# First block's input projection of a fused two-block model: features as the outer loop in its first half

## The chip, the cores and the metric

One NeuronCore of a Trainium2 chip. The metric is the device time of one execution in microseconds. The whole program is one launch on one core; its inputs lie in HBM.

## The reference, cut to what matters

The program computes two "first blocks" (pooling and convolution mixers with adaptive modulation), then an FFN, a sparse attention mixer, two FFNs, a difference attention mixer and a last FFN, all for 256 tokens of width 1024. The change touches the first of the two first blocks (l = 0) alone:

```python
c_act = jax.nn.silu(c)                              # (1, 1024)
mod = c_act @ w_ada[l] + b_ada[l]                   # (1, 3072)
shift, scale, gate = jnp.split(mod, 3, axis=-1)
h = rms_norm(x, g_pre[l]) * (1.0 + scale[:, None, :]) + shift[:, None, :]
proj = h @ w_in[l]                                  # (1, 256, 3072)
u_a, b_a, c_a, gate_a, u_p, gate_p = jnp.split(proj, 6, axis=-1)
y_a = b_a * causal_depthwise_conv(c_a * u_a, w_conv[l]) * jax.nn.silu(gate_a)
y_p = causal_multiscale_pool(u_p, w_pool[l], pool_scale[l]) * jax.nn.silu(gate_p)
y = jnp.concatenate([y_a, y_p], axis=-1) @ w_out[l]
x = x + gate[:, None, :] * rms_norm(y, g_post[l])
```

## The kernel before, in words

**Precision.** Every large product is made of three passes in a fast f32 format: high part of the weight by high part of the activation, high by low, low by high. ScalarE makes the high part of a weight chunk (`split_hi`, L745: a copy into `whi`), VectorE the low part (`split_lo`, L1349: the difference into `wlo`). Small products (sums, transposes) are plain f32.

**The stream of weights.** `stream_items` (L90) writes out the order of all loads. Each item is 1 MiB and goes into one of three slots of `raw` (RAW = 3, L41). SyncE issues load r when `raw_done` has reached r - 2, which means that item r - 3 has been released (L433). Releases come from VectorE, in the order of the items: the low split of a weight chunk, or, for rows of `w_ada`, the multiplication by a scalar of `cact` and the addition to a row of sums in SBUF (`add_row`, L1355 and L1356; called from `accumulate_ada`). ScalarE needs for a high split that the chunk has landed and that TensorE is done with the chunk three before (`chunk_used`); TensorE needs the low split. VectorE, ScalarE and TensorE work their programs in order, so a release or a split that is ready still waits for what stands ahead of it in its engine's queue.

**Block 1 before.** The first 8 items are the rows of `w_ada[0]` for shift and scale (128 x 2048 each, rows of 8 KB). VectorE adds them up; TensorE sums the 128 partitions by 16 matmuls against ones (L2291), which gives all 16 columns of shift and scale; `modulation(0, 0)` (L1529 to L1531) makes shift and gain. Meanwhile x lands as the fourth transfer, ScalarE squares and scales it (L896, L901), GpSimd takes the power -0.5 (L516), TensorE transposes x (`turn`, L2087). ScalarE then applies gain and shift (`to_features`, L793), VectorE makes the high and low parts `hT_hi`, `hT_lo` (L1565, L1566). `keep_clock` (L2281) puts 3 and 2 matmuls of 512 f32 columns around the sums, whose result nobody reads.
The projection goes by 12 chunks of 256 columns of W_in, all 1024 features deep (rows of 1 KB), in the order of `IN1_ORDER`: 48 matmuls a chunk (`pooled_pair` for the first two, `cols_by_tokens` for the rest, L2122 to L2124), into rotating PSUM banks. After chunks there are hooks: windowed means of the pooling branch (L2314, L2315, they need `win_ready` from GpSimd), the mixing (L2321), the sums of the gate (L2273) and its spread over the partitions (L2330); on ScalarE the evictions, `gate` diagonal (L940) and taps; on VectorE `pooled_y` parts (L1583), the convolution (L1605) and the gating. From the third chunk on, the stream has after every chunk one item for later: 4 items of gate rows and 8 rows of `w_ada[1]`. The output product (`out_chunk` L2221 to L2223, `out_pair` L2239 to L2241) uses 4 chunks of W_out, 24 matmuls of 512 columns each. After it, `sum_modulation(1, 0)` opens block 2 on TensorE.

Of the kernel before, what the change touches and what calls it, by code (L numbers as in the profile page):

```python
# [57 lines left out]
SIDE_CHUNKS = (2, 3, 4, 5, 6, 7, 8, 9)  # L58
SIDE_OUT = (0, 1, 2, 3)
GATE_CHUNKS = (2, 3, 4, 5)  # L60

# [28 lines left out]
def stream_items():  # L90


    items = [("ada", 0, kt) for kt in range(KD)]
    side = [("gate", 0, c) for c in range(4)] + [("ada", 1, kt) for kt in range(KD)]
    for n, c in enumerate(IN1_ORDER):
        items.append(("w", "in1", 0, c))
        if n in SIDE_CHUNKS:
            items.append(side.pop(0))
    for n, c in enumerate(OUT1_ORDER):
        items.append(("w", "out1", 0, c))  # L100
        if n in SIDE_OUT:
            items.append(side.pop(0))
    assert not side
# [29 lines left out]
def two_blocks_kernel(nc, a, out):  # L133
    ctx = ExitStack()
    with ctx:
# [57 lines left out]
        y1 = region[:, 3072:5120].rearrange("p (k t) -> p k t", t=T)  # L193
        pooled = region[:, 5120:6144].rearrange("p (g t) -> p g t", t=T)
# [82 lines left out]
        shift_rows = sem("shift_rows")  # L277
# [81 lines left out]
        def source(item):  # L359
            if item[0] == "ada":  # L360
                return a["w_ada"][item[1]][item[2] * P:(item[2] + 1) * P, 0:2 * D].rearrange("(k p) n -> p k n", p=P)
# [3 lines left out]
            kind, *at = item[1:]  # L365
            if kind == "in1":
                return col_chunk(a["w_in"][at[0]], at[1] * CC)
# [16 lines left out]
        def size(item):  # L384
            return 8 * NGATE if item[1:] == ("nsa", 10) else CH

        def raw_view(slot, ap):
            k, n = ap.shape[1], ap.shape[2]
            return raw[:, slot, 0:k * n].rearrange("p (k n) -> p k n", k=k)
# [31 lines left out]

        def landed_value(r, it=0):

            return it * (16 * 6 // RAW) + 16 * (r // RAW + 1)
# [5 lines left out]
        def _(sp):  # L430
            def load(r):
                if r >= RAW:
                    sp.wait_ge(raw_done, r - RAW + 1)  # L433
                src = source(items[r])
                sp.dma_start(raw_view(r % RAW, src), src).then_inc(raw_landed[r % RAW], 16)
# [22 lines left out]
            while r < len(items):  # L458
# [3 lines left out]
                else:  # L462
                    if r == RAW:
# [10 lines left out]
        def _(pool):  # L474
# [11 lines left out]
            nc.gpsimd.memset(ones[:, :], 1.0).then_inc(consts_ready, 1)  # L486

            for at, name in ((A_GPRE, "g_pre"), (A_GPOST, "g_post"), (A_F1, "ffn1_norm_2"), (A_MIX, "mix_norm_2"),
# [7 lines left out]
            pool.dma_start(rowsB[B_BADA:B_POS, :], a["b_ada"].rearrange("l (k p) -> (l k) p", p=P))\  # L496
               .then_inc(params_landed, 16)
            pool.dma_start(rowsB[B_POS:B_NQ, :], a["nsa_cmp_pos_2"][0].rearrange("v (m j) d -> (v m) (j d)", j=2))\
               .then_inc(params_landed, 16)
            n_params = 9  # L500
# [56 lines left out]
            def count_windows():  # L557

                pool.wait_ge(colsd_ready, 2)
# [8 lines left out]
            pool.wait_ge(raw_done, KD - 1)  # L568
# [160 lines left out]
        def _(act):  # L729
# [5 lines left out]
            act.dma_start(rowsC[:, :], a["c"].rearrange("b (k p) -> (b k) p", p=P)).then_inc(c_landed, 16)  # L735

# [44 lines left out]
            def to_features(l, tt=None, hf=None):  # L781

                b = turn_base(l, 1)
                for kt in range(KD) if hf is None else range(4 * hf, 4 * hf + 4):
                    if kt % 4 == 0:
                        act.wait_ge(turned, kt // 4 + 1 if tt is None else 2 + 2 * tt + kt // 4 + 1)
# [103 lines left out]
            nc.scalar.activation(lam_s[:, 7:8], acc[:, 7, 0:1], ACT.Copy).then_inc(silu_ready, 1)  # L890
            for l in range(2):

                if l == 0:
                    act.wait_ge(x_landed, 16)
                    for tt in range(TT):
                        step(nc.scalar.activation(scratch[:, tt * D:(tt + 1) * D], x[:, tt, :], ACT.Square,  # L896
                                                  scale=D ** -0.5, accum_out=stat[:, tt:tt + 1]))
                        act.sem_inc(ss_ready, 1)
                    for tt in range(TT):
                        act.wait_ge(rs_ready, tt + 1)  # L900
                        nc.scalar.activation(xn[:, tt, :], x[:, tt, :], ACT.Copy, scale=rs[:, tt:tt + 1])\  # L901
                          .then_inc(xn_ready, 1)
                    split_to(w_at[("in1", l, IN1_ORDER[0])])
                    act.wait_ge(diag_ready, 1)
                    to_features(l)
                else:
                    act.wait_ge(diag_ready, 4)
# [5 lines left out]
                for n, c in enumerate(IN1_ORDER):  # L913
                    w = w_at[("in1", l, c)]
# [6 lines left out]
                    if n == 3:  # L921
                        act.wait_ge(u_ps, l + 1)
                        for tt in range(TT):
                            nc.scalar.activation(pooled[:, 2 * tt:2 * tt + 2, :],
                                                 acc[:, 4 + tt, :].rearrange("p (g t) -> p g t", t=T),
                                                 ACT.Copy).then_inc(u_ready, 1)
                    if n == 6:
                        act.wait_ge(z_ready, l + 1)
                        tap = A_CONV + 12 * l + 8
                        for g in range(4):  # L930
                            nc.scalar.activation(v1[:, g, :], z1[:, g, :], ACT.Copy,
                                                 scale=colA[:, tap + g:tap + g + 1]).then_inc(tap_ready, 1)
# [2065 lines left out]
```

## Time and profile before

| | us |
|---|---|
| median of 3 runs | 1285.74 |
| lowest, highest | 1283.43, 1291.79 |
| the profiled execution, its own time | 1283.65 |
| its span in the trace | 1281.9 |
| TensorE matmul busy | 1246.6 (97%) |
| VectorE busy | 887.8 (69%) |
| ScalarE busy | 641.3 (50%) |
| GpSimd busy | 171.9 (13%) |

A page and a trace were taken in the profiled execution; times in them count from the span's start, and the span leaves out 1.75 us of the execution's own time. The ends of matmuls are modelled, so the distance between their starts is the pace, not the duration. PE is TensorE's matmul, PEld its weight load, DVE VectorE, ACT ScalarE, POOL GpSimd, SP SyncE. `x6` at the end of a row of the timeline means six instructions in one row; an f32 matmul leaves two records.

### The profile page before, as it was taken

How to read it: one execution, taken by the hardware profiler on the slowest of the kernel's cores; microseconds unless marked ns; L12 is line 12 of the kernel's file. 1: busy time of each engine (PE TensorE's matmuls, PEld its weight loads, DVE VectorE, ACT ScalarE, POOL GpSimd, SP SyncE). 2: the span in 40 equal slices, each digit the busy share in tenths (PEclk: the TensorE clock that was granted, in tenths of full speed). 3: DMA queues.
4: the chain of work that ended last, by engine and by line, in shares of the span. 5: the costliest groups of instructions: out<-in, count | busy, mean ns of one | idle time of the engine just before them, and what ended most of it. 6: DMA issues, size and time to landing. Idle time of an engine off the chain costs nothing.

```text
span 1281.9 us, 19570 instructions
## 1 busy us (share of the span) xinstructions
PE 1246.6 (97%) x7756; PEld 1109.8 (87%) x7756; DVE 887.8 (69%) x931; ACT 641.3 (50%) x825; POOL 171.9 (13%) x217
## 2 busy tenths in 40 slices
PE   3899999999999999989999999999999999999998
PEld 2899899888888899978988888888889998988887
DVE  5779666676666767987766667666667787766665
ACT  2445545554444456855544444444446675644442
POOL 8400100088200120000100001000001221200000
PEclk9999899999999999999999999999999999999999
DMA  9897495455556462314555654655554444455551
GB/s 361 262 324 270 158 326 185 145 197 183 186 189 196 121 215 66 132 67 131 187 182 189 196 186 144 227 197 191 182 186 164 148 147 157 151 187 196 196 196 66
DMA packets 166816, 236.88 MB, mean 185 GB/s; under 512 B 5140, under 2 KB 146592, under 8 KB 164704
## 3 DMA queue, kind: packets, MB, share of 16 engines
q1 hardware_dynamic: 165920, 235.09, 54.9%
q0 software_dynamic: 816, 0.89, 0.3%
q8 instruction: 45, 0.74, 0.2%
q14 instruction: 19, 0.16, 0.0%
q10 hardware_dynamic: 16, 0.00, 0.0%
HBM read 234.92 MB, written 1.05 MB: 184 GB/s over the span
## 4 chain that ended last, share of the span: by engine, by line
PE 85%; DVE 6%; DMA 4%; ACT 2%; POOL 1%; issue 1%; DVEq 0%; ACTq 0%; POOLq 0%
PE acc L2185 23%; PE acc L2187 12%; PE acc L2221 5%; PE acc L2222 5%; PE acc L2223 5%; PE acc L2203 4%; PE acc L2204 3%; PE acc L2205 3%; DVE wlo L1349 2%; DMA raw<-in_w_ada_dram 2%; PE acc L2239 2%; PE acc L2593 2%; DMA raw<-in_w_in_dram 2%; PE acc L2241 2%; PE acc L2240 2%; PE acc L2122 2%
## 5 line engine op out<-in xcount | busy, mean ns | idle before, releaser
L1349 DVE TENSOR_TENSOR wlo<-raw,whi 128x2048 fp32r<-128x2048 f32 (+1 forms) x199 | 453.8, 2283 | 199.7 <-ACT whi L745 198.7
L745 ACT ACTIVATE whi<-raw 128x2048 fp32r<-128x2048 f32 (+1 forms) x199 | 378.1, 1904 | 184.3 <-PE acc L2223 113.1
L2185 PE MATMUL acc<-hT,whi 128*128 128x512 f32 x1280 | 320.2, 392 | 0.5 <-ACTq L826 0.5
L2185 PEld LDWEIGHTS acc<-hT,whi 128*128 128x128 f32 x1280 | 232.4, 189 | 43.9 <-issue 0.7
L2187 PEld LDWEIGHTS acc<-hT,wlo 128*128 128x128 f32 x1280 | 174.6, 190 | 12.5
L2187 PE MATMUL acc<-hT,wlo 128*128 128x256 f32 x1280 | 178.5, 282 | 0.0
L2221 PE MATMUL acc<-whi,sT_hi 128*128 128x512 f32 x320 | 125.0, 391 | 0.0
L2222 PE MATMUL acc<-wlo,sT_hi 128*128 128x512 f32 x320 | 125.0, 390 | 0.0
L2223 PE MATMUL acc<-whi,sT_lo 128*128 128x512 f32 x320 | 124.5, 389 | 0.0
L2203 PE MATMUL acc<-whi,hT 128*128 128x256 f32 x416 | 120.2, 289 | 1.1 <-DVE hT L1423 1.1
L2204 PE MATMUL acc<-wlo,hT 128*128 128x256 f32 x416 | 117.6, 283 | 0.0
L2205 PE MATMUL acc<-whi,hT 128*128 128x256 f32 x416 | 117.5, 283 | 0.0
L807 ACT ACTIVATE region<-acc 128x512 f32<-128x512 f32 x40 | 23.9, 598 | 142.9 <-PE acc L2187 142.9
L2122 PE MATMUL acc<-hT,whi 128*128 128x256 f32 x320 | 92.1, 288 | 0.0
L2124 PE MATMUL acc<-hT,wlo 128*128 128x256 f32 x320 | 90.5, 283 | 0.0
L2123 PE MATMUL acc<-hT,whi 128*128 128x256 f32 x320 | 90.5, 283 | 0.0
L535 POOL TENSOR_SCALAR ms<-stat 128x1 f32<-128x1 f32 x12 | 12.5, 1044 | 549.6 <-ACTq L764 549.4
L2203 PEld LDWEIGHTS acc<-whi,hT 128*128 128x128 f32 x416 | 79.5, 191 | 3.8 <-issue 1.8
L2204 PEld LDWEIGHTS acc<-wlo,hT 128*128 128x128 f32 x416 | 79.7, 191 | 0.2
L2205 PEld LDWEIGHTS acc<-whi,hT 128*128 128x128 f32 x416 | 79.6, 191 | 0.0
L1449 DVE TENSOR_TENSOR region<-acc,region 128x512 f32<-128x512 f32 x40 | 27.6, 691 | 73.8 <-ACT region L807 72.7
L2223 PEld LDWEIGHTS acc<-whi,sT_lo 128*128 128x128 f32 x320 | 60.1, 188 | 12.8
(324 smaller groups left out, 1950.6 us busy)
## 6 DMA issues: line engine op xcount, KB each, us to landing
raw<-in_ffn_w_in_dram SPq DMA_DIRECT2D x88, 1024.0 KB, 5.1
raw<-in_ffn_w_out_dram SPq DMA_DIRECT2D x44, 1024.0 KB, 5.0
raw<-in_w_ada_dram SPq DMA_DIRECT2D x24, 1024.0 KB, 5.9
raw<-in_w_in_dram SPq DMA_DIRECT2D x24, 1024.0 KB, 5.9
raw<-in_diff_w_in_dram SPq DMA_DIRECT2D x12, 1024.0 KB, 5.2
raw<-in_nsa_w_in_dram SPq DMA_DIRECT2D x10, 1024.0 KB, 5.3
raw<-in_w_out_dram SPq DMA_DIRECT2D x8, 1024.0 KB, 4.9
raw<-in_nsa_cmp_w_dram SPq DMA_DIRECT2D x4, 1024.0 KB, 5.5
```

The costliest lines, as they stand in the source:

```text
L745: nc.scalar.activation(whi[:, w % SPL, 0:n], raw[:, r % RAW, 0:n], ACT.Copy).then_inc(hi_ready, 1)
L1349: nc.vector.tensor_tensor(wlo[:, w % SPL, 0:n], raw[:, r % RAW, 0:n], whi_f[:, w % SPL, 0:n], ALU.subtract).then_inc(raw_done, 1)
L2122: nc.tensor.matmul(o, hi[:, kt, cs], hT_hi[:, kt, :], start=kt == 0, stop=False)
L2123: nc.tensor.matmul(o, hi[:, kt, cs], hT_lo[:, kt, :], start=False, stop=False)
L2185: nc.tensor.matmul(o, hi[:, kt, cs], hT[:, :, kt, :], start=kt == 0, stop=False)
L2187: ins = nc.tensor.matmul(o[:, 0:T], lo[:, kt, cs], hT_hi[:, kt, :], start=False, stop=kt == KD - 1)
L2203: nc.tensor.matmul(o, hT_hi[:, kt, ts], hi[:, kt, :], start=kt == 0, stop=False)
L2204: nc.tensor.matmul(o, hT_hi[:, kt, ts], lo[:, kt, :], start=False, stop=False)
L2205: ins = nc.tensor.matmul(o, hT_lo[:, kt, ts], hi[:, kt, :], start=False, stop=kt == KD - 1)
L2221: nc.tensor.matmul(o, sh, hi[:, k, ns], start=start and k == 0, stop=False)
L2222: nc.tensor.matmul(o, sh, lo[:, k, ns], start=False, stop=False)
L2223: ins = nc.tensor.matmul(o, sl, hi[:, k, ns], start=False, stop=stop and k == 1)
```

## The change

The order of the first items becomes: pair 0, row 0, pair 1, rows 1 and 2, pair 2, rows 3 and 4, pair 3, rows 5, 6 and 7, then gate rows 0, and the six other column chunks (`COLS1`) with gate rows and rows of `w_ada[1]` between them. There are 38 items before block 2 in place of 36, with the same bytes.

- A **pair** is the part of `w_ada[0]` that gives shift and scale of two feature tiles (256 features): 1024 x 2 x 256, in two halves of 1 MiB, in runs of 1 KB, two DMAs a half. Pairs 0 and 1 are multiplied on TensorE (`pair_product`: 16 f32 matmuls of one column a half, with `cact` as the moving operand; a matmul with zeros opens the four columns); VectorE passes their release on when TensorE is done (`pass_pair`). Pairs 2 and 3 are added up on VectorE by pieces of 512 (`add_pair`), and TensorE sums them (`sum_pair`).
- A **row** is 128 features of W_in by 1536 columns (gate_a, u_p, gate_p), 0.75 MiB. `row_high` and `row_low` accumulate it over the features in banks 4 and 5 (tokens by u_p) and 0 to 3 (four gates), whose accumulation `clear_gates` opens with four f32 matmuls of 512 columns by zeros. `row_last` closes the banks.
- x is loaded first; the transposed x is copied out of PSUM (`xT`), and ScalarE applies gain and shift to one pair of feature tiles at a time (`features`), between the splits of the rows; `features_lo` on VectorE makes the low part.
- `keep_clock` is gone. `b_ada` and `g_pre` are loaded from ScalarE's queue and transposed first, the other parameters later (`turn_params`). GpSimd loads the pooling weights after 16 releases (before: 7), and corrects the windows after that.
- The hooks (means, mixing, gate, taps) are the same operations at other places between the six column chunks. Block 2 and all behind it are unchanged.

```diff
+NPAIRS = KD // 2
+PE_PAIRS = 2
+ROW0, ROWN = 3 * CW, 3 * CW
+ROW_GATES = ((6, 0), (7, 1), (10, 2), (11, 3))
+COLS1 = ((0, 7), (1, 6), (4, 0), (5, 1), (2, 2), (3, 3))
...
-    items = [("ada", 0, kt) for kt in range(KD)]
...
+    items = pair(0) + rows(0) + pair(1) + rows(1, 2) + pair(2) + rows(3, 4) + pair(3) + rows(5, 6, 7)
+    side = {0: [("gate", 0, 1)], 1: [("gate", 0, 2)], 2: [("gate", 0, 3)], 3: [("ada", 1, 1)], 4: [("ada", 1, 2)]}
+    items.append(("gate", 0, 0))
+    for n, (c, _) in enumerate(COLS1):
         items.append(("w", "in1", 0, c))
+        if n == 0:
+            items.append(("ada", 1, 0))
+        items += side.get(n, [])
...
-            pool.wait_ge(raw_done, KD - 1)
+            pool.wait_ge(raw_done, 2 * NPAIRS + KD)
...
+            act.wait_ge(x_landed, 16)
+            square_x(0)
+            square_x(1)
+            act.wait_ge(rs_ready, 1)
+            nc.scalar.activation(xn[:, 0, :], x[:, 0, :], ACT.Copy, scale=rs[:, 0:1]).then_inc(xn0_ready, 1)
...
+            features(0)
+            split_to(0)
+            split_to(1)
+            features(1)
+            split_to(2)
+            split_to(3)
+            features(2)
+            split_to(4)
+            split_to(5)
+            features(3)
+            b0 = w_at[("in1", 0, COLS1[0][0])]
+            split_to(b0 + 1)
+            act.wait_ge(rows_done, 1)
+            nc.scalar.activation(p0[:, :, :], acc[:, 4:6, :], ACT.Copy).then_inc(proj_ready, 2)
+            for c, b in ROW_GATES:
+                evict_row_gates(c, b)
+            split_to(b0 + 2)
+            evict_cols(0, 7)
...
+            def pass_pair():
+
+                for _ in range(2):
+                    if raw_at[0]:
+                        dve.wait_ge(raw_done, raw_at[0])
+                    raw_at[0] += 1
+                    dve.wait_ge(pair_used, raw_at[0] if raw_at[0] < 3 else raw_at[0] - 1)
+                    dve.sem_inc(raw_done, 1)
...
+            nc.vector.tensor_scalar(xn[:, 1, :], x[:, 1, :], rs[:, 1:2], None, ALU.mult).then_inc(xn_ready, 1)
+            for hf in range(2):
+                dve.wait_ge(turned, 3 + hf)
+                nc.vector.tensor_copy(turn_bank(xT, 1, hf), acc[:, 2 + hf, :].rearrange("p (k t) -> p k t", t=P))\
+                  .then_inc(xT_ready, 1)
+            pass_pair()
+            pair_modulation(0)
+            features_lo(0)
+            row_lo(1)
+            pass_pair()
+            row_lo(1)
+            pair_modulation(1)
+            row_lo(1)
+            features_lo(1)
+            add_pair(2)
+            row_lo(1)
+            pair_modulation(2)
+            row_lo(1)
+            features_lo(2)
+            add_pair(3)
+            row_lo(1)
+            pair_modulation(3)
+            features_lo(3)
+            row_lo(2)
...
+            pair_product(0, 0)
             turn(0, 0)
             turn(0, 1)
-            pe.wait_ge(raw_done, KD - 2)
-            keep_clock(3)
...
+            pair_product(0, 1)
+            clear_gates()
+            row_high(0, False)
+            row_high(0, True)
+            pair_product(1, 0)
+            row_low(0)
+            pair_product(1, 1)
+            turn_params()
+            row_high(1, False)
+            row_high(1, True)
+            row_low(1)
...
+            row_high(3, False)
+            sum_pair(2)
+            row_high(3, True)
...
+            row_last(7)
...
+            pe.wait_ge(colsd_ready, 2)
+            cols1(0)
+            pe.wait_ge(proj_ready, 2)
+            pooled_means(0)
+            cols1(1)
+            pe.wait_ge(proj_ready, 3)
+            cols1(2)
+            pe.wait_ge(proj_ready, 8)
+            mix_pooled(0)
+            sum_modulation(0, 1)
+            cols1(3)
+            cols1(4)
+            spread_gate(0)
+            cols1(5)
```

On VectorE, behind the rows, the low splits of the first four column chunks and their side items come first, then the gate's modulation (it waits for `sum_modulation(0, 1)`), and the parts of y between the next splits.

## Rows read from the trace of the kernel before

**Rows 1.** The page, busy tenths of 40 slices of 32 us: TensorE and the DMA engines.

```profile
PE   3899999999999999989999999999999999999998
...
DMA  9897495455556462314555654655554444455551
```

**Rows 2.** Timeline of TensorE: start, duration, line, tiles, count, idle before.

```profile
37.16 0.36 PE L2134 MATMUL acc<-whi,hT 128*128 128x256 f32 x1 [2.09 <-DVE hT L1566]
...
140.06 4.79 PE L2273 MATMUL acc<-ones,region 128*128 128x1 f32 x32
```

**Rows 3.** Timeline of TensorE, 40 to 60 us, single matmuls of 256 columns.

```profile
41.26 0.41 PE L2134 MATMUL acc<-whi,hT 128*128 128x256 f32 x1
41.47 0.41 PE L2135 MATMUL acc<-whi,hT 128*128 128x256 f32 x1
...
52.11 0.28 PE L2123 MATMUL acc<-hT,whi 128*128 128x256 f32 x1
52.23 0.28 PE L2124 MATMUL acc<-hT,wlo 128*128 128x256 f32 x1
```

**Rows 4.** Windows: stretch, busy us (count) of PE, PEld, DVE, ACT, POOL; PEclk, DMA share, GB/s.

```profile
40.00:45.00 5.00, 4.63 (x28) 4.34 (x27) 5.00 (x3) 1.81 (x2) 4.77 (x4) 0.67 0.22 39
...
120.00:130.00 10.00, 10.00 (x46) 8.29 (x45) 7.86 (x5) 3.48 (x3) 0.00 (x0) 1.00 0.85 324
```

**Rows 5.** Chain of work that ended last, 0 to 160 us: start, us, what.

```profile
57.82 6.81 DMA raw<-in_w_in_dram
64.66 1.92 ACT whi L745
66.67 2.29 DVE wlo L1349
...
69.52 1.30 DVE region L1356
...
123.33 5.40 DMA raw<-in_w_out_dram
```

**Rows 6.** Timeline of SyncE's queue, 0 to 175 us.

```profile
42.86 0.37 SPq L435 DMA_DIRECT2D raw<-in_w_ada_dram  x1
...
123.33 0.37 SPq L435 DMA_DIRECT2D raw<-in_w_out_dram  x1
```

**Rows 7.** Waits of SyncE's queue, 0 to 160 us: total us, times, longest.

```profile
SPq L435 <- DVE wlo L1349: 82.9, 18, 16.3
```

**Rows 8.** Waits of all engines, 0 to 160 us, same columns.

```profile
PE acc L2239 <- DVE wlo L1349: 0.6, 1, 0.6
```

**Rows 9.** Timeline of all engines, the start.

```profile
6.29 1.28 DVE L1355 TENSOR_SCALAR region<-raw,cact 128x2048 f32<-128x2048 f32 x1 [6.29 <-DMA raw<-in_w_ada_dram]
...
8.94 2.35 DVE L1356 SCALAR_TENSOR_TENSOR region<-raw,cact,region 128x2048 f32<-128x2048 f32 x1 [1.36 <-DMA raw<-in_w_ada_dram]
...
16.23 0.58 POOL L516 TENSOR_TENSOR rs<-ms,power 128x1 f32<-128x1 f32 x1
...
21.11 1.97 PE L2087 MATMUL acc<-ident,xn 128*128 128x128 f32 x8 [0.87 <-ACT xn L901]
```

**Rows 10.** Groups by line and form, 0 to 160 us: busy, mean ns, idle before.

```profile
L1349 DVE TENSOR_TENSOR wlo<-raw,whi 128x2048 fp32r<-128x2048 f32 x19 | 43.6, 2305 | 17.5 <-ACT whi L745 17.0 <-DVE region L1356 0.2 <-DVE region L1583 0.2
L745 ACT ACTIVATE whi<-raw 128x2048 fp32r<-128x2048 f32 x19 | 36.3, 1919 | 40.8 <-DMA raw<-in_w_in_dram 33.3 <-DMA raw<-in_w_out_dram 7.2 <-ACT scratch L955 0.4
...
L1356 DVE SCALAR_TENSOR_TENSOR region<-raw,cact,region 128x2048 f32<-128x2048 f32 x13 | 30.5, 2349 | 6.2 <-DMA raw<-in_w_ada_dram 6.0
...
L793 ACT ACTIVATE region<-acc,shift,gain 128x256 f32<-128x256 f32 x8 | 3.8, 578 | 1.8 <-DVEq L1534 1.8
```

**Rows 11.** Timeline of TensorE, f32 matmuls of 512 columns and of one.

```profile
24.30 5.49 PE L2281 MATMUL acc<-xn,ones 128*128 128x512 f32 x6 [1.22 <-DVE region L1356]
...
33.19 1.88 PE L2281 MATMUL acc<-xn,ones 128*128 128x512 f32 x4
...
85.11 1.84 PE L2273 MATMUL acc<-ones,region 128*128 128x1 f32 x16
```

More of the change, by code:

```diff
@@ L384, in size @@
         def size(item):
+            if item[1] == "row":
+                return ROWN
             return 8 * NGATE if item[1:] == ("nsa", 10) else CH
         def raw_view(slot, ap):
+            if len(ap.shape) == 4:
+                return raw[:, slot, :].rearrange("p (k s n) -> p k s n", k=ap.shape[1], s=ap.shape[2])
             k, n = ap.shape[1], ap.shape[2]
@@ L420, in pair_bank, with transfers @@
             return (6 if l == 0 else 2) if c == 0 else 0
+        def transfers(r):
+            return 2 if items[r][0] == "pair" else 1
         def landed_value(r, it=0):
-            return it * (16 * 6 // RAW) + 16 * (r // RAW + 1)
+            return it * (16 * 6 // RAW) + sum(transfers(q) for q in range(r % RAW, r + 1, RAW)) * 16
         block = ctx.enter_context(nc.Block())
@@ L434, in load @@
                 src = source(items[r])
+                if items[r][0] == "pair":
+                    for s in range(2):
+                        sp.dma_start(raw_view(r % RAW, src)[:, :, s, :], src[:, :, s, :]).then_inc(raw_landed[r % RAW], 16)
+                    return
                 sp.dma_start(raw_view(r % RAW, src), src).then_inc(raw_landed[r % RAW], 16)
@@ new lines, in pair_product @@
+            def pair_product(f, half):
+                r = items.index(("pair", f, half))
+                pe.wait_ge(raw_landed[r % RAW], landed_value(r))
+                rv = raw[:, r % RAW, :].rearrange("p (k s n) -> p k s n", k=4, s=2)
+                if half == 0:
+                    nc.tensor.matmul(acc[:, 6, 4 * f:4 * f + 4], zeros[:, :], ones[:, 0:4], start=True, stop=False)
+                for j in range(4):
+                    for k in range(4):
+                        kt = 4 * half + k
+                        ins = nc.tensor.matmul(acc[:, 6, 4 * f + j:4 * f + j + 1],
+                                               rv[:, k, j // 2, (j % 2) * P:(j % 2 + 1) * P], cact[:, kt:kt + 1],
+                                               start=False, stop=j == 3 and kt == KD - 1)
+                ins.then_inc(pair_used, 1)
+                if half:
+                    pe.wait_ge(pair_used, 2 * f + 2)
+                    pe.sem_inc(pair_ps, 1)
@@ new lines, in pooled_means @@
+            def pooled_means(l):
+                pe.wait_ge(wsmall_landed, 48)
+                pe.wait_ge(win_ready, 1)
+                for g in range(4):
+                    o, gs = acc[:, 4 + g // 2, (g % 2) * T:(g % 2) * T + T], slice(g * P, (g + 1) * P)
+                    nc.tensor.matmul(o, p0[:, 0, gs], win0[:, g, :], start=True, stop=False)
+                    ins = nc.tensor.matmul(o[:, P:T], p0[:, 1, gs], win1[:, g, :], start=False, stop=True)
+                ins.then_inc(u_ps, 1)
```

470 lines of the change are left out of this document (322 added, 148 removed).

## The prediction, made before the change was run

> **What bounds the kernel now.** I read the page's slices first. TensorE is busy at nine tenths or more in nearly every slice, and the first slice is the exception, while the DMA engines are full in the first four slices and at about half later [rows 1]. The change rebuilds block 1 only, so the question is what sets the end of block 1.
>
> TensorE's timeline answers it. The first projection matmul starts at 37.16 us, and the sums of block 2's modulation, which follow the last output matmul of block 1, start at 140.06 us [rows 2]. In between it works almost without a gap; the one wait in the output product is 0.6 us [rows 8]. Its work there: 12 chunks of 48 matmuls of 256 columns, 0.12 us apart [rows 3], are 69.1 us; 4 output chunks of 24 matmuls of 512 columns at 0.227 us (46 in 10 us, [rows 4]) are 21.8 us; windowed means 2.5, mixing 1.5, gate sums 1.7 and gate spread 1.8 us are 7.5 us. That is 98.4 us, and 37.2 + 98.4 = 135.6; the other 4.5 us are a slow start and the wait. So the stage is bound by TensorE from 37 us on, and what looks free is its idle start.
>
> The second bound lies close behind it. The chain of waits doesn't run over TensorE but over the stream of weights: a transfer (6.81), the high split on ScalarE (1.92), the low split on VectorE (2.29), an add on VectorE (1.30), again a transfer [rows 5]. Three raw slots serve it, and load r is issued when item r-3 is released, in VectorE's order: SyncE waited 82.9 us for low splits alone in the first 160 us [rows 7]. Item 16 is issued at 57.82 and item 34, the last output chunk, at 123.33 [rows 5, 6]: 3.6 us an item. Whoever wants block 1 to end sooner must get 36 items through three slots sooner, not only start TensorE sooner.
>
> **The change part by part, with its prices.**
> Loads: one transfer of 1 MiB with little else under way takes 5.40 us to land [rows 5]; the first two items landed 2.65 us apart, 6.29 and 8.94 [rows 9]. I take 2.1 us fixed and 3.2 us of transfer for a half pair or a chunk with rows of 1 KB, and for a row of W_in of 0.75 MiB 2.1 + 2.1. Bounds: 4.9 and 6.8 us.
> Splits: 1.92 and 2.31 us for 2048 columns [rows 10], so 1.44 and 1.74 for the 1536 of a row.
> Adds on VectorE: 2.35 us for 2048 columns [rows 10], 1.30 for 1024 [rows 5], which by a straight line gives 0.77 for 512; four of them a half pair, about 5.7 us a pair. Two pairs are 11.5 us, where eight rows before were 18; this saving is real, but lies inside the chain below.
> Products of one column on TensorE (two pairs, 64 and 2 zeros): 16 such sums took 4.65 us at 140.06 [rows 2], 8 took 1.70 (1.84 with the last one's end) at 85.11 [rows 11]. That is 0.21 to 0.29 us each: a half pair is 3.4 to 4.8 us. I take 4.8 for the first two and 4.1 later.
> Clearing four banks: four f32 matmuls of 512 columns, each two records. Six such records took 5.49 us at 24.30, four took 1.88 at 33.19 [rows 11]: 3.6 to 6.8 us. I take 6.8, since here too only transposes and thin products run before them.
> A row of W_in: three passes, each 2 matmuls of 512 and 8 of 256 columns, 2 x 0.227 + 8 x 0.12 = 1.42 us. Eight rows are 34.1 us; six chunks before were 34.6. Nothing is gained in matmuls.
> Features of a pair on ScalarE: four operations, about 2.2 us (0.58 for one of 256 columns, [rows 10]); their low parts on VectorE 0.8.
>
> **The start, step by step.** x is now first and lands near 5.7, the halves of pair 0 near 8.9 and 12.1, row 0 at 14.2. Two squares end at 8.5; GpSimd has issued its parameters by 11.3 (two fewer), so its power, 0.58 [rows 9], gives the first factor at 12.3. TensorE multiplies half 0 from 9.0 to 13.7, turns x (1.97 a tile, [rows 9]) to 17.7 and multiplies half 1 to 22.5. But slot 0 is released by VectorE, and that release stands in its queue behind the copies of tile 1, at 18.5. So item 3 is issued at 18.5 and lands at 23.8, item 4 at 22.7 and lands at 28.0. From 14.2 to about 20 nothing is under way, where the DMA engines of the kernel before are full [rows 1].
> The first modulation is ready at 23.3, its features at 25.5; only then does ScalarE split row 0, which had landed at 14.2: high 26.9, low 28.7, item 5 issued, landing at 33.0. TensorE clears to 29.3, makes the two high passes to 32.2, half (1,0) to 36.3, the low pass to 37.7 and half (1,1) to 41.8. Each half holds its slot until then: items 6, 7 and 8 are issued at 36.5, 42.0 and 43.8. The kernel before issues item 11 at 42.86 [rows 6]. The second modulation is ready at 44.3.
> Then a cycle closes over VectorE and ScalarE, from one modulation to the next: features 2.2, high split 1.4, low split 1.7, low features 0.8, adds 5.7, low split 1.7, modulation 0.65, handovers 0.2, in sum 14.4 us for 3.5 MiB. Two cycles: 58.7 and 73.1. TensorE has 9.5 us of work in each and stands idle for the rest.
> After 73.1: features 2.2, high 1.4 and low 1.7 of row 6: 78.6, when item 17, the first column chunk, is issued. 5.3 + 1.9 + 2.3 later TensorE may multiply it, at 88.2 (row 7 was done at 85.4).
> From there its work is 6 x 5.76 + 7.5 + 21.8 = 63.9 us: 152.1. Added to this are waits. The means need p0, whose copy stands on ScalarE behind the high split of the second chunk, not landed before 93.6: 2.6. The spread of the gate waits for ScalarE's diagonal, behind an eviction and a split: 2.3. The gate row: 0.8. Of the output chunks the last three come late, 3.8 + 4.1 + 1.7, as item 36 isn't issued before 153: 19 items after item 17 at 3.9 us each. It is more than the 3.6 of before, because VectorE's queue now holds a wait for the gate's sums (3.7 us, behind chunk 3 on TensorE; the loads stand behind it) and one for the high part of y (3.9). Sum: 152.1 + 15.3 = 167.4 us against 140.1 in the same place before, or 27 us more. The same recurrences on the kernel before end at 136.6, 3.5 too early, which would make it 31; I take 28.
>
> **What costs nothing.** The two parameters moved to ScalarE's queue land before half 0 does. The pooling weights now wait for 16 releases, at 80 us, and GpSimd's window corrections come behind them (10 us before); ready near 92, needed at 96. If that cover of 4 us is gone, the means wait for the rest. Block 2 starts from the same state, its first slots filled while the sums run, so the shift goes through to the end undiminished.
>
> **Sum.** The profiled execution took 1283.65 us (span 1281.9), 2.1 below the median of the runs. 1283.65 + 28 = 1311.7: I predict 1312 us.
>
> **Rivals.**
> (a) TensorE stays the bound and the slots keep up: not slower. From 29.3 us on it would have 34.1 (rows), 8.2 (pair 1), 2.0 (sums of pairs 2 and 3), 0.8 and 63.9: 138.3, so 1.8 us less than before, 1282 us. It needs half a pair released within 4 us of landing and splits that don't wait for features. For it speaks that nearly 40 us of idle TensorE are there to be used; against it that the chain of before runs over the slots [rows 5]. It decides if a cycle takes under 10 us in place of 14.4.
> (b) The row stage is as I say, but the second half waits for nothing: 152.1, 12 us more, 1296 us. For it: before, the one wait in the outputs was 0.6 us [rows 8]; against it: the slots are then ahead, here they are behind.
> (c) The array runs at half clock through the row stage. Before, while matmuls came with gaps from 37 us on, the granted clock fell to 0.67 in the slice 40 to 45 [rows 4], and a matmul of 256 columns then took 0.21 us, at 1.2 GHz, in place of 0.12 [rows 3]. A pass would be 2.7 us, a cycle of TensorE 17, above the other two engines' 14.4; the recurrences then end 11 us later, at 1323 us.
> The Trainium skill, "TensorE: Matmul & The Clock Gate", section "Loop structure matters more than you think", says that waiting for a DMA between bursts of matmuls lets the clock drop for the next burst. By that rule (c) would be the likeliest; the trace agrees at 40 us, and doesn't show a longer stage of this kind.
>
> **How the numbers follow.** My case 0.60, (b) 0.16, (c) 0.15, (a) 0.09. Own range of the likeliest: 1303 (thin products at 0.21, clearing at 3.6, faster loads) to 1317. The range for 8 in 10 takes in (b) and (c): 1296 to 1324. A measurement of this kernel can tell about 1% from no change, 13 us. (a) and half of (b) fall within it: 0.13; faster by over 1% is 0.02; slower 0.85.
>
> **What would show it.** Right: the first row matmul near 27 to 30 us, issues of items 3 and 4 near 18 and 23, modulations some 14 us apart, low splits that end there, column chunks from 85 to 90, block 2's sums near 168. The DMA share falls below 0.7 between 15 and 80 us. Wrong: row passes without gaps from 30 us on and the first column chunk before 76, or output chunks back to back.

## The result, and the profile after

The changed kernel takes 1325.88 us (median of 4 runs, 1324.34 to 1327.84) against 1284.83 for the kernel before (4 runs beside it, 1283.43 to 1291.79): a ratio of 1.031, 95% interval 1.027 to 1.035. It is slower by 41 us; 28 were forecast, and 1324 was the top of the range. The direction and the place were right, the size was not.

Page of the kernel after, busy tenths of 40 slices (33 us each). TensorE's first slice is 7 in place of 3, but the next five (9, 7, 9, 7, 8) aren't full either, up to 198 us; the DMA engines are at 5 in the first two slices, where they were at 9 and 8 [rows 1].

```profile
PE   7979789999999999999999999999999999999998
...
DMA  5588659546555544341455555455554542555551
```

Timeline of TensorE after, the start (two records are one f32 matmul). L2498 is a pair product on TensorE, L2312 the turning of x, L2612 the clearing of the banks, L2526 and L2540 the 512-column matmuls of a row pass.

```profile
9.69 6.96 PE L2498 MATMUL acc<-cact,raw 128*128 128x1 f32 x32
16.52 3.65 PE L2312 MATMUL acc<-ident,xn 128*128 128x128 f32 x16
19.97 6.83 PE L2498 MATMUL acc<-cact,raw 128*128 128x1 f32 x32
27.09 5.89 PE L2612 MATMUL acc<-xn,region 128*128 128x512 f32 x8 [0.30 <-PE acc L2498]
32.42 1.02 PE L2526 MATMUL acc<-whi,hT 128*128 128x512 f32 x2
...
35.77 4.59 PE L2498 MATMUL acc<-cact,raw 128*128 128x1 f32 x32
40.23 1.20 PE L2540 MATMUL acc<-wlo,hT 128*128 128x512 f32 x2
42.93 6.82 PE L2498 MATMUL acc<-cact,raw 128*128 128x1 f32 x32
```

Four half pairs take 6.96 + 6.83 + 4.59 + 6.82 = 25.2 us, and 17.8 had been taken for them. TensorE works almost without a gap up to 49.75 us, where its forecast ended at 41.8. Of these 8 us the products are 7.4. Its first product began 0.7 late, and the low pass of row 0, from 40.23 to 42.93, took 2.7 us in place of 1.4; against that, turning and clearing were 1.8 shorter than their terms (3.45 and 5.33 us from start to start, 4.0 and 6.8 had been taken).

Timeline of VectorE after, the gain of each pair's modulation, in the order of the pairs:

```profile
27.20 0.16 DVE L1677 SCALAR_TENSOR_TENSOR gain<-mod,colA 128x2 f32<-128x2 f32 x1
51.82 0.16 DVE L1677 SCALAR_TENSOR_TENSOR gain<-mod,colA 128x2 f32<-128x2 f32 x1
65.88 0.16 DVE L1677 SCALAR_TENSOR_TENSOR gain<-mod,colA 128x2 f32<-128x2 f32 x1
80.07 0.16 DVE L1677 SCALAR_TENSOR_TENSOR gain<-mod,colA 128x2 f32<-128x2 f32 x1
```

The first is 3.9 us later than forecast (23.3), the second 7.5 (44.3), and from there the two cycles are 14.1 and 14.2 us, where 14.4 was forecast. The lateness is complete at 51.8 us and is carried on.

Timeline of TensorE after, the second half: the rows that begin with a wait. The first column chunk (L2347, forecast at 88.2) starts at 95.32, and block 2's sums, which started at 140.06 before [rows 2], at 179.75.

```profile
95.32 0.35 PE L2347 MATMUL acc<-hT,whi 128*128 128x256 f32 x1 [2.77 <-DVE wlo L1475]
...
138.66 1.98 PE L2593 MATMUL acc<-xn,ones 128*128 128x512 f32 x4 [1.69 <-ACT xn L989]
...
156.12 0.79 PE L2433 MATMUL acc<-whi,sT_hi 128*128 128x512 f32 x1 [4.09 <-DVE wlo L1475]
...
165.69 0.50 PE L2451 MATMUL acc<-whi,sT_hi 128*128 128x512 f32 x1 [1.43 <-DVE wlo L1475]
...
172.82 0.50 PE L2451 MATMUL acc<-whi,sT_hi 128*128 128x512 f32 x1 [2.75 <-DVE wlo L1475]
...
179.75 3.63 PE L2602 MATMUL acc<-ones,region 128*128 128x1 f32 x32
```

With 2.95 us before the means (L2577), the waits behind the first column matmul are 12.9 us; the output chunks, which waited 0.6 before [rows 8], now wait 8.3. Windows of the kernel after, same columns as [rows 4]; at 0.50 a slice was at half clock throughout, at 0.66 for 3.4 of 5 us:

```profile
40.00:45.00 5.00, 5.00 (x23) 4.81 (x23) 0.00 (x0) 0.00 (x0) 0.00 (x0) 0.50 0.50 157
45.00:50.00 5.00, 4.75 (x23) 4.66 (x22) 0.11 (x1) 0.00 (x0) 0.00 (x0) 0.50 0.00 0
50.00:55.00 5.00, 4.95 (x20) 4.59 (x21) 1.94 (x4) 2.87 (x5) 0.00 (x0) 0.50 0.83 268
...
95.00:100.00 5.00, 4.68 (x27) 4.71 (x27) 1.73 (x3) 0.00 (x0) 0.72 (x2) 0.66 0.97 349
100.00:110.00 10.00, 7.05 (x40) 6.28 (x39) 7.29 (x5) 5.75 (x7) 0.00 (x0) 0.83 0.91 294
...
150.00:160.00 10.00, 5.91 (x18) 4.44 (x18) 9.80 (x9) 1.23 (x2) 0.00 (x0) 0.72 0.52 190
160.00:170.00 10.00, 8.57 (x34) 6.39 (x33) 7.92 (x4) 3.47 (x2) 0.00 (x0) 0.94 0.88 330
```

From the first column matmul to block 2's sums are 84.4 us: 63.9 of work at full pace by the forecast's list, 12.9 of waits, and 7.6 left over. Most of the left-over falls where the clock does. At or soon after the waits of 2.77, 2.95 and 4.09 us TensorE works at half pace for 3.4, 3.4 and some 5.2 us, which costs half of these 12 us, 6.0. The waits of 1.69, 1.43 and 2.75 us show no such fall, and 1.6 of the 7.6 us stay open.

**The account.** Block 2's sums came 39.7 us later than before (179.75 - 140.06). Of these the forecast's recurrences had 27.3 (167.4 - 140.06). The first column chunk is 7.1 later than in them (95.32 against 88.2), and the stretch behind it 5.2 longer (84.4 against 167.4 - 88.2 = 79.2). These three make up the 39.7 by construction; what lies behind the last two is for the experiments. In block 2 the first chunk of plain columns starts 39.3 us later than before (202.19 against 162.93), so what follows adds only 1 or 2 us.

### The profile page after: what moved, and what is told of

It is laid out like the page before. It is cut to its first block, busy times and chain, and to the rows that moved or that the text cites. A ratio compares the mean times of both kernels' runs of the same rounds, so it can differ in the third digit from the quotient of the medians.

```text
span 1323.2 us, 19771 instructions
## 1 busy us (share of the span) xinstructions
PE 1276.7 (96%) x7824; PEld 1136.1 (86%) x7824; DVE 883.5 (67%) x954; ACT 644.3 (49%) x835; POOL 156.9 (12%) x216
## 4 chain that ended last, share of the span: by engine, by line
PE 82%; DVE 5%; ACT 3%; DMA 3%; POOL 1%; issue 1%; ACTq 0%; DVEq 0%; POOLq 0%
PE acc L2397 22%; PE acc L2399 12%; PE acc L2433 5%; PE acc L2434 5%; PE acc L2435 5%; PE acc L2415 3%; PE acc L2416 3%; PE acc L2417 3%; DMA raw<-in_w_in_dram 2%; DVE wlo L1475 2%; PE acc L2948 2%; PE acc L2347 2%; PE acc L2348 2%; PE acc L2349 2%; PE acc L2451 1%; PE acc L2452 1%
## 5 line engine op out<-in xcount | busy, mean ns | idle before, releaser
L2399 PE MATMUL acc<-hT,wlo 128*128 128x256 f32 x1280 | 178.5, 282 | 0.0
L2347 PE MATMUL acc<-hT,whi 128*128 128x256 f32 x256 | 74.8, 292 | 3.8 <-DVE wlo L1475 3.8
L2433 PEld LDWEIGHTS acc<-whi,sT_hi 128*128 128x128 f32 x320 | 60.9, 190 | 16.3 <-DVE wlo L1475 4.5
L2349 PE MATMUL acc<-hT,wlo 128*128 128x256 f32 x256 | 73.1, 286 | 0.0
L2348 PE MATMUL acc<-hT,whi 128*128 128x256 f32 x256 | 73.1, 285 | 0.0
```

Source lines behind the costliest of these rows:

```text
L2347: nc.tensor.matmul(o, hi[:, kt, cs], hT_hi[:, kt, :], start=kt == 0, stop=False)
L2348: nc.tensor.matmul(o, hi[:, kt, cs], hT_lo[:, kt, :], start=False, stop=False)
L2399: ins = nc.tensor.matmul(o[:, 0:T], lo[:, kt, cs], hT_hi[:, kt, :], start=False, stop=kt == KD - 1)
L2433: nc.tensor.matmul(o, sh, hi[:, k, ns], start=start and k == 0, stop=False)
```

## The experiments

Theory P: the four half-pair products on TensorE, which ran at half clock and had been priced too low, made the first half longer than forecast. Theory S: the second half is bound by the slots and VectorE's queue, not by TensorE. The rivals were that the clearing, the slots alone or ScalarE's order set the start, and that TensorE with its half clock sets the second half. Differences are to the kernel after unless said otherwise; kernels with few runs are compared by their trace marks, since the times of one kernel lie 3.5 us apart after the change and up to 13 in x5_four.

**x1_warm**: TensorE is kept busy ahead of the first product.

```diff
+            for _ in range(28):
+                nc.tensor.matmul(acc[:, 0, 0:P], ones[:, :], ones[:, :], start=True, stop=True)
             pe.wait_ge(early_landed, 32)
```

> 28 f32 matmuls of 128 columns (ones by ones, result unused) are put on TensorE before the first parameters are waited for, in time that it spends idle; nothing else differs from the changed kernel. Theory P (the products of one column are slow because the array stands at half clock, whatever the rows say of the granted clock): the first half of pair 0 falls from 6.96 us to about 3.5, the second half falls back, since thin products don't hold the clock; second modulation near 49.5 in place of 51.6, first column chunk near 93, total 2 to 3 us less. Theory S (slots and queue order alone matter, product time is fixed by something else, as reading weights straight from the landed slot): the first half stays at 6.9 and nothing moves.

Measured: 1330.2 us. Timeline of TensorE:

```profile
2.54 9.45 PE L2477 MATMUL acc<-ones 128*128 128x128 f32 x56
...
12.52 4.22 PE L2500 MATMUL acc<-cact,raw 128*128 128x1 f32 x32
20.05 6.83 PE L2500 MATMUL acc<-cact,raw 128*128 128x1 f32 x32
```

The same 16 products take 4.22 us behind the warming block and 6.96 without it; the second half pair, behind the turning of x, is back at 6.83. So the product's price is a matter of the clock, as theory P had it. The earlier marks and the gain of 2 to 3 us that it forecast didn't come. The block delayed the first product by 2.8 us, so its end (16.6) and the second gain (51.93, 49.5 forecast) stayed where they were. The first column chunk came 2.4 later, at 97.70 (sums at 184.22): the two cycles from the second gain on took 15.7 and 15.0 us here; x6_drop below shows why.

**x2_vector_pairs**: pairs 0 and 1 are added up on VectorE as pairs 2 and 3 are.

```diff
-PE_PAIRS = 2
+PE_PAIRS = 0
...
-            pass_pair()
+            add_pair(0)
...
-            pair_product(0, 0)
...
-            pair_product(0, 1)
+            sum_pair(0)
```

> Pairs 0 and 1 are added up on VectorE like pairs 2 and 3 (pair 0 before x is scaled), and TensorE only sums them; four half products of 5.3 to 7.0 us leave TensorE. Theory P (the products on TensorE and the slots that they hold are the loss of the first 50 us): second modulation near 33 in place of 51.6, first column chunk near 77 in place of 95.3, block 2's sums near 160, total 18 us less, about 1308. Theory S, in its strict form (the order of queues costs the time, whoever adds up): less than 6 us.

Measured: 1309.99 us, 16 less. Timeline of VectorE, the same four gains:

```profile
20.27 0.21 DVE L1677 SCALAR_TENSOR_TENSOR gain<-mod,colA 128x2 f32<-128x2 f32 x1
33.78 0.16 DVE L1677 SCALAR_TENSOR_TENSOR gain<-mod,colA 128x2 f32<-128x2 f32 x1
47.85 0.16 DVE L1677 SCALAR_TENSOR_TENSOR gain<-mod,colA 128x2 f32<-128x2 f32 x1
62.94 0.16 DVE L1677 SCALAR_TENSOR_TENSOR gain<-mod,colA 128x2 f32<-128x2 f32 x1
```

The step from the first gain to the second is 13.5 us here and 24.6 in the kernel after; the later ones stay at 14 to 15. The first column chunk starts at 78.04, 17.3 earlier, the sums at 162.05, 17.7 earlier. These marks are within some 2 us of those that theory P had forecast (33, 77 and 160). The use of TensorE for the pairs, which was to relieve VectorE, costs 16 us of the 41 by the medians. The ratio to the kernel before is 1.018 (1.008 to 1.029). At block 2's plain columns it is 16.4 us as well (185.78), between the two profiled executions only 12.8.

**x3_order**: ScalarE makes a row's high split ahead of the features of the pair, not behind.

```diff
-            features(0)
             split_to(0)
+            features(0)
             split_to(1)
-            features(1)
             split_to(2)
+            features(1)
```

> On ScalarE each high split of a row stands before the features that it stood behind (split 0, features 0, splits 1 and 2, features 1, splits 3 and 4, and so on); no work is added or removed. If the cycle of 14.1 us is closed by features and high split in one chain, as I say: cycles of about 12 us, first column chunk near 90 in place of 95.3, block 2's sums near 174, total 5 to 6 us less. If VectorE's own work or the loads set the cycle: below 1 us.

Measured: 1323.38 us; gains at 27.17, 51.83, 66.70 and 77.84, first column chunk at 91.98, sums at 178.28. The second gain doesn't move at all: up to there neither ScalarE's order nor a row's split decides. The last one comes 2.2 us earlier. Half of what was forecast came (column chunk near 90, sums near 174, 5 to 6 us in all). Of 3.3 us at the first column chunk 1.5 are left at the sums, a first sign that the second half has a bound of its own.

**x4_modlate**: VectorE waits for the gate's sums one chunk later.

```diff
+                    stream_to(b0 + 4)
                     modulation(0, 1)
                     lambda_parts()
-                    stream_to(b0 + 4)
```

> On VectorE the wait for the gate's sums moves behind the next side item and low split (one line moved). If the 5.7 us that VectorE stood there are what holds the loads of the second half back: nothing changes to the first column chunk (95.3), block 2's sums near 175 in place of 179.75, total 4 to 5 us less. If the second half is bound by something else: within 1 us.

Measured: 1324.97 us, sums at 176.32 (3.4 earlier). First the kernel after, then this one, timeline of VectorE at the gate's modulation:

```profile
117.29 2.29 DVE L1475 TENSOR_TENSOR wlo<-raw,whi 128x2048 fp32r<-128x2048 f32 x1 [1.44 <-ACT whi L792]
125.24 0.17 DVE L1747 TENSOR_TENSOR mod<-acc,colB 128x8 f32<-128x8 f32 x1 [5.66 <-PE acc L2602]
```

```profile
123.49 2.29 DVE L1475 TENSOR_TENSOR wlo<-raw,whi 128x2048 fp32r<-128x2048 f32 x1 [1.08 <-ACT whi L792]
125.70 0.16 DVE L1747 TENSOR_TENSOR mod<-acc,colB 128x8 f32<-128x8 f32 x1
```

The wait of 5.66 us is gone, and of it 3.4 us are gained at the sums and still at block 2's plain columns (198.81 against 202.19), near the 4 to 5 that were forecast; the output chunks wait 2.0 and 5.5 us, 7.4 in all in place of 8.3. The time hardly moves, so the gain is lost behind the part that was changed.

**x6_drop and x7_before_drop**: in both kernels six of the eight rows of `w_ada[1]` are left out of the computation, so that block 2's shift and scale lack their share.

```diff
+    items = [it for it in items if not (it[0] == "ada" and it[1] == 1 and 1 <= it[2] <= 6)]
```

> Leaves out of the computation six of the eight rows of w_ada[1] (kt 1 to 6), so block 2's shift and scale lack their share; six items fewer go through the three slots between the first column chunk and block 2. Theory: the second half of block 1 is bound by slots and VectorE's queue, so the first column chunk stays at 95 us, and block 2's sums come at 167 in place of 179.75 (recurrences: 12 to 13 earlier), total about 1313. Rival: the second half is bound by TensorE and the half clock; then dropping loads changes nothing, sums at 178 to 180, total 1325.

> The kernel before with the same six rows of w_ada[1] left out of the computation. Theory: before, the slots kept just ahead of TensorE, so dropping six items moves block 2's sums by 1 us at most, from 140.06 to 139 or 140, and the total by as little (1283 to 1285). Rival: the stream set the end of block 1 before as well; then the sums come 6 x 3.6 = up to 20 us earlier, 120 to 130, and the total at 1265 to 1275.

Measured: 1317.15 and 1282.98 us. Timelines of TensorE, block 2's sums, the changed kernel first:

```profile
165.44 3.63 PE L2603 MATMUL acc<-ones,region 128*128 128x1 f32 x32
```

```profile
139.19 4.25 PE L2274 MATMUL acc<-ones,region 128*128 128x1 f32 x32
```

Six loads fewer bring the sums 14.3 us earlier after the change and 0.9 before it, while the first column chunk nearly stays (94.66 and 95.32); from there to the sums it is 13.7 us less (70.8 against 84.4). This is the clearest result of the study: the same stretch of the program, bound by TensorE before, is bound by the slots and VectorE after. The six rows take their additions on VectorE with them, so this doesn't part the slots from VectorE's queue. Of the 14.3 us 13.1 reach block 2's first plain columns (189.11), and 8.7 the total. Between 500 and 900 us, far behind the change, the granted clock of this run was 0.97, of the kernel after 1.00. x2_vector_pairs (0.97) and x4_modlate (0.98) also lose 3 to 4 us between block 2's plain columns and the end of their profiled executions; that the clock there took them is likely and not shown.

This run shows one thing more. Its first half is the changed kernel's, operation for operation, yet its second half pair cost 4.04 us in place of 6.83; x11_after_tailconv, with the same first half, has 4.01. Timelines of TensorE and of VectorE in x6_drop:

```profile
16.64 3.29 PE L2313 MATMUL acc<-ident,xn 128*128 128x128 f32 x16
19.76 4.04 PE L2499 MATMUL acc<-cact,raw 128*128 128x1 f32 x32
...
62.63 1.70 PE L2511 MATMUL acc<-ones,region 128*128 128x1 f32 x8
```

```profile
48.89 0.16 DVE L1678 SCALAR_TENSOR_TENSOR gain<-mod,colA 128x2 f32<-128x2 f32 x1
...
64.37 0.16 DVE L1675 TENSOR_TENSOR shift<-acc,colB 128x2 f32<-128x2 f32 x1 [1.57 <-PE acc L2511]
```

The second gain comes 2.9 us earlier for it (48.89, and 48.96 in x11_after_tailconv, in place of 51.82). But only 0.7 and 1.6 us of that reach the first column chunk. Here the clock was at half again in the row stage (0.54 from 60 to 65 us, where the kernel after has 1.00); the pair's sums took 1.70 us in place of 0.95, VectorE waited 1.57 us for them, and the cycle took 15.7 us, the next 14.9. So the clock at a given place differs between executions of the same operations, and moves a mark in the first half by 1 to 3 us.

**x8_release**: VectorE releases the first half of pair 0 before it copies the turned x (`pass_half` is `pass_pair` for one half).

```diff
+            pass_half()
             for hf in range(2):
                 dve.wait_ge(turned, 3 + hf)
...
-            pass_pair()
+            pass_half()
             pair_modulation(0)
```

> VectorE passes on the release of the first half of pair 0 before it copies the transposed x, not behind it. Theory of the slots alone: item 3 is issued 2 to 3 us earlier than 20.27 and every later mark follows, total 1322 to 1323. Theory that the products on TensorE set the start (6.96, 6.83, 5.89, 4.59, 6.82 us in a row): item 3 is issued near 17, but the second modulation stays within 0.5 us of 51.82 and the total within 1 us of 1325.5.

Measured: 1324.99 us. Timelines of SyncE's queue and of TensorE:

```profile
16.74 8.30 SPq L477 DMA_DIRECT2D raw<-in_w_ada_dram  x4
```

```profile
19.96 4.08 PE L2507 MATMUL acc<-cact,raw 128*128 128x1 f32 x32
24.34 5.35 PE L2621 MATMUL acc<-xn,region 128*128 128x512 f32 x8 [0.30 <-PE acc L2507]
...
40.14 6.82 PE L2507 MATMUL acc<-cact,raw 128*128 128x1 f32 x32
```

Item 3 is issued at 16.74 (20.27 after), and the second gain comes at 49.03 in place of 51.82. That looks like the slots' theory, but it isn't: x6_drop and x11_after_tailconv have their second gain at 48.89 and 48.96, with item 3 issued at 20.02 and 20.14. What the three have in common is a second half-pair product of 4.0 to 4.1 us in place of 6.83. So the earlier release moved the issue by 3.3 us and, as far as these marks show, nothing behind it, as theory P had it; the first column chunk too (93.63) is where x11_after_tailconv has it (93.74). At the sums 0.2 us are left of 1.7 (179.51).

**x5_four**: the edits of x2, x3 and x4 together, and ScalarE copies `p0` and the row gates before it splits the second column chunk.

```diff
             b0 = w_at[("in1", 0, COLS1[0][0])]
-            split_to(b0 + 1)
+            split_to(b0)
             act.wait_ge(rows_done, 1)
...
                 evict_row_gates(c, b)
+            split_to(b0 + 1)
             split_to(b0 + 2)
```

> Four edits together: pairs 0 and 1 on VectorE, ScalarE's high splits ahead of the features, VectorE's wait for the gate sums one item later, and ScalarE evicting p0 and the row gates before it splits the second column chunk. My recurrences with the measured prices: second, third and fourth modulation at 31.6, 44.3 and 55.8 us (after: 51.8, 65.9, 80.1), first column chunk on TensorE at 70.5 (after: 95.3), block 2's sums at 146, plus up to 5 for half clock in the gaps: 146 to 151, so 1290 to 1295 us in all. If the slots set only the row stage and TensorE the rest, the sums come at 70.5 + 64 = 135 and the total is 1279. If the edits do not add up, because x2_vector_pairs already took all there was, the sums stay at 160 and the total at 1308.

Measured: 1296.78 us (median of 4; ratio to before 1.012, 1.006 to 1.017), 29 less than after. Second to fourth gain at 32.70, 48.08 and 59.04, first column chunk at 73.12, sums at 151.49; the recurrences had 31.6, 44.3, 55.8, 70.5 and 146 to 151. That is more than 16 + 2.5 + 0.9 us, what three of the edits gave alone; by the sums' marks it is 28.3 against 17.7 + 1.5 + 3.4 = 22.6. Part of the excess may be the clock's; the fourth was not run alone, so it stays open how much is its own and how much x3_order's and x4_modlate's edits gain once other waits are gone. From the first column chunk to the sums are 78.4 us, still 14.5 above TensorE's 63.9; timeline of TensorE, the two waits in the output:

```profile
127.89 0.50 PE L2435 MATMUL acc<-whi,sT_hi 128*128 128x512 f32 x1 [1.44 <-DVE wlo L1477]
...
138.02 0.80 PE L2453 MATMUL acc<-whi,sT_hi 128*128 128x512 f32 x1 [4.37 <-DVE wlo L1477]
```

**x9_tail and x10_tailconv**: x5_four with two rows of `w_ada[1]` fewer ahead of the last W_out, and that with VectorE's convolution behind its second split of W_out.

```diff
-        items += {0: [("ada", 1, 3)], 1: [("ada", 1, 4), ("ada", 1, 5)], 2: [("ada", 1, 6)],
-                  3: [("ada", 1, 7)]}[n]
+        items += {0: [("ada", 1, 3)], 1: [], 2: [("ada", 1, 4)],
+                  3: [("ada", 1, 5), ("ada", 1, 6), ("ada", 1, 7)]}[n]
...
+                    stream_to(b0 + 7)
                     convolve(0)
...
-                    stream_to(b0 + 7)
```

> x5_four with two rows of w_ada[1] fewer ahead of the last chunk of W_out (rows 5, 6 and 7 behind it, row 4 ahead of it). Stream theory: x6_drop moved block 2's sums 14.3 us earlier for six items, 2.4 each; here the last W_out is two items earlier, so its product ends some 5 us earlier, but the three rows behind it now reach the sums last: block 2's sums at 147 to 148 in place of 151.49, total 1292 to 1293. Rival: the half clock and the waits for y set the outputs, and the order of the loads changes nothing: sums 151, total 1297.

> x9_tail with VectorE splitting the second chunk of W_out before the convolution of y, not behind it. In x5_four the convolution and its product by b_a (5.35 us) stood ahead of that split, and three slots waited for them. Theory that VectorE's queue order is what costs the second half: the second output chunk waits for nothing (1.4 us before), the third less than 3 us (4.4 before), block 2's sums at 143 to 145, total 1288 to 1290. Rival: the third output chunk needs y's convolution in any case, so the wait moves there whole, and the sums stay where x9_tail has them.

Measured: 1296.10 us (1.008, 1.005 to 1.011) and 1299.45 us (1.012, 1.007 to 1.017). Timelines of TensorE, x9_tail first:

```profile
149.12 5.57 PE L2604 MATMUL acc<-ones,region 128*128 128x1 f32 x32 [1.99 <-DVEq L1500]
156.34 1.97 PE L2314 MATMUL acc<-ident,xn 128*128 128x128 f32 x8 [1.66 <-DVE xn L1531]
```

```profile
134.74 0.50 PE L2453 MATMUL acc<-whi,sT_hi 128*128 128x512 f32 x1 [2.63 <-DVE wlo L1477]
139.33 0.50 PE L2453 MATMUL acc<-whi,sT_hi 128*128 128x512 f32 x1 [0.19 <-DVE wlo L1477]
148.96 5.33 PE L2604 MATMUL acc<-ones,region 128*128 128x1 f32 x32 [2.51 <-DVEq L1500]
```

In x9_tail the last two W_out chunks no longer wait. In x10_tailconv the second doesn't wait and the third waits 2.63 us in place of 4.37, as forecast. The sums start 2.4 and 2.5 us earlier than in x5_four, but now they wait for the additions behind the output and run partly at half pace (5.57 and 5.33 in place of 3.63 us), and the plain columns of block 2 start at 174.66 and 174.62, against 173.84 in x5_four. Neither gives anything; the totals forecast, 1292 to 1293 and 1288 to 1290, and x10_tailconv's sums at 143 to 145 failed. In these two orders the wait moved from the output to behind it.

**x11_after_tailconv**: x4_modlate's, x9_tail's and x10_tailconv's edits of the second half on the changed kernel, its first half untouched.

> The same three edits of order in the second half (gate sums' wait one item later, convolution behind the second split of W_out, two rows of w_ada[1] behind the last W_out) on the changed kernel, its first half untouched. If the halves are independent: first column chunk at 95.3 as before, block 2's sums 8 to 10 us earlier than 179.75, 170 to 172, total 1316 to 1318. If x6_drop's gain came from the missing work on VectorE and not from the order, the sums stay within 4 us of 179.75.

Measured: 1319.43 us (one run; 1316 to 1318 forecast), sums at 170.83, 8.9 earlier. The number is the one forecast, but 1.6 of it are there at the first column chunk already (93.74), through the clock in the first half; the second half itself gave 7.3. At block 2's plain columns 5.4 are left (196.80). So the order matters, and not only the work that x6_drop took away. That a late stream is helped by it and one nearly on time (x5_four) isn't is a reading of three runs, not tested by itself.

No version beat the kernel before; x9_tail and x5_four come nearest.

## Why the prediction was wrong in size

- **What bounds the kernel before**: right. x7_before_drop moved the sums by 0.9 us when six loads were taken out, so TensorE set the end, with the stream just behind it.
- **The start step by step**: its structure was right (the products hold their slots, a stretch without transfers, items 3 and 4 late), its marks 1.8 to 7.5 us early. Items 3 and 4 were issued at 20.27 and 26.86 against 18.5 and 22.7. The DMA share was below 0.7 only up to 50 us, not up to 80: from 50 to 80 it was 0.75 to 0.85.
- **The step that failed: "That is 0.21 to 0.29 us each ... I take 4.8 for the first two and 4.1 later."** A product of one column took 0.43 us (6.96 / 16) in three of the four half pairs, outside the range that was given. The row of [rows 2], 4.79 us for 16, was taken as the highest price; it is a mixture, since the clock fell while it ran (0.73 in the slice from 140 to 145 us). x7_before_drop has the same sums in 4.25 us, after and x5_four in 3.63, x9_tail in 5.57: one operation, four prices. The bound above should have been twice the price at full clock (2 x 0.21), as the columns of [rows 3] were doubled. It is 7.4 us on TensorE (25.2 against 17.8). The second gain was 7.5 late and the first column chunk 7.1; with the low pass of row 0 at half clock (1.3) and the late first product (0.7) on one side and the clearing and turning, taken 1.8 too long, on the other, the products are the bulk of it. How much of a cheaper product arrives depends on the clock in the row stage too: in x6_drop and x11_after_tailconv the four cost 21.9 us, and the first column chunk still came 6.5 and 5.5 us behind the forecast. The saving of additions on VectorE that stood against it lay inside the chain, as forecast; x2_vector_pairs shows that the exchange cost 16 us.
- **The cycle of 14.4 us**: right (14.1, 14.2) where the clock stood at full; 15.7 and 14.9 in x6_drop, where it didn't. Rival (a), which needed under 10 us, fell.
- **Rival (c), half clock through the row stage**: the clock was at half from 40 to 55 us and back at 0.95 and 1.00 afterwards, so its condition held in part. In this execution its price came through the products and one row pass of 2.7 us. In x1_warm, x6_drop and x11_after_tailconv, where the clock fell again in the row stage, TensorE did stretch a cycle, to 15.6 or 15.7 us; the 17 of (c) never came.
- **The second half**: the waits were forecast at 15.3 us in all and measured 12.9, in the places named (means, gate spread, output chunks), and x6_drop shows the cause, the stream. Missing was what a wait does to the clock: the 63.9 us of work took 71.5, of which 6.0 are work at half pace and 1.6 open. This is the term that was set to nothing, and with waits 2.4 us shorter than forecast 5.2 us net of the error. The items took 4.1 us each (from 85.52, item 17, to 163.34, item 36), near the 3.9 forecast; it was their start that was late.
- **The range**: its top came from (c) alone. Two terms, both mostly from the half clock, erred in the same direction, 7.1 and 5.2 us; with them the forecast of 1312 becomes 1324, where the profiled execution has 1324.95. A range that adds the half-clock price to every thin product and behind the long waits would have reached it.
- **The 28 us**: choosing 28 between the 27 of the marks and the 31 of the recurrences' difference was harmless beside this.

## What to carry to other kernels

A product of one column has two prices, one at each level of the clock (0.21 and 0.43 us here). Work out the range with both; a row that took a value in between may be a mixture and is no bound. Compare such marks over several executions before you credit an edit with 2 or 3 us: the same operations had a mark at 51.8 in some and at 48.9 in others. Moving a sum from a busy engine to an idle one gains only if the slot that feeds it comes free sooner: here each 1 MiB half was held by TensorE through up to 7 us of products and everything queued ahead of them, where VectorE adds up a whole pair in 6.1 us (57.81 to 63.95 in the kernel after). To learn whether a stretch is bound by its loads, take some loads out in both kernels and compare one mark: 14.3 against 0.9 us said it, where the waits alone looked like many small causes.

## What the runs showed of the hardware

The granted clock of the record can't be trusted before its first change. In the kernel after it stands at 1.00 from 10 to 30 us, while the products run at 0.43 us each, the pace of half clock; in x1_warm, where it had changed before, it reads 0.50 from 20 to 30 us for the same products at the same pace (6.83 us for 16). Windows of the kernel after, then of x1_warm:

```profile
10.00:20.00 10.00, 10.00 (x49) 10.00 (x49) 1.39 (x2) 2.34 (x3) 8.58 (x22) 1.00 0.38 130
20.00:30.00 10.00, 9.70 (x37) 8.09 (x37) 1.98 (x7) 2.49 (x5) 0.63 (x2) 1.00 0.53 163
```

```profile
20.00:30.00 10.00, 9.70 (x38) 8.09 (x37) 2.06 (x7) 2.40 (x5) 0.55 (x2) 0.50 0.49 160
```

The pace, the distance of the starts of equal matmuls, is the better reading. Also, the clock fell while one-column products ran: the row passes before them ran at full pace (32 to 35 us), and the third half pair, 4.59 us, is a mixture that ends at half clock, where the next pass starts (two 512-column records in 1.20 us, against 0.63 before).

And the clock at a place isn't fixed by the program. The second half pair, behind the same operations, took 6.83 us in the kernel after, x3_order and x4_modlate, and 4.04 and 4.01 us in x6_drop and x11_after_tailconv.
